# Two attention stages of a decoder step: the turns of the probabilities and the products with the values, spread over other slots of a round

## What is computed

```
# group B (MLA), sample: all 2048 cached latents (128 wide) and rotary keys (32 wide), and the 8 new ones
s = (einsum('bqhr,bkr->bhqk', ql, c_kv) + einsum('bqhd,bkd->bhqk', qp, k_pe)) * scale
p = softmax(where(key_pos <= q_pos, s, -inf));  o_lat = einsum('bhqk,bkr->bqhr', p, c_kv)
# group A (DSA), sample: an indexer scores the keys, each query keeps its best 256
score = einsum('bqh,bqhk->bqk', w_idx, relu(einsum('bqhd,bkd->bqhk', q_idx, k_idx)))
_, sel = top_k(score, 256)
p = softmax(einsum('bqhd,bqkd->bqhk', q, k[sel]) / 8);  o_a = einsum('bqhk,bqkd->bqhd', p, v[sel])
```

## Time and profile before

| what | us |
|---|---|
| median of three runs | 3161.12 |
| the profiled execution | 3156.46 |
| its span, first to last instruction | 3154.7 |
| PE busy | 2939.6 (93%) |
| DVE busy | 1413.7 (45%) |
| ACT busy | 998.4 (32%) |
| POOL busy | 643.3 (20%) |

### The profile page before, as it was taken

One profiled execution on the slowest core, in us unless ns is written; L12 is line 12 of the kernel. 1 busy time (PEld: TensorE's weight loads), 2 busy tenths in 40 slices (PEclk: granted clock), 3 DMA queues, 4 the chain that ended last, 5 costly groups with the idle time before them and its releaser, 6 DMA issues. The chain is left out here.

```text
span 3154.7 us, 45592 instructions
## 1 busy us (share of the span) xinstructions
PE 2939.6 (93%) x18282; PEld 2524.9 (80%) x18298; DVE 1413.7 (45%) x2118; ACT 998.4 (32%) x1620; POOL 643.3 (20%) x562
## 2 busy tenths in 40 slices
PE   7999999888898899999999999998888988999997
PEld 7999879755566689998799997795656666999975
DVE  2222255579764442223632223735887445222236
ACT  2222233454443332222422222334444333122223
POOL 1111021330113141110221110412302123211103
PEclk9999999999999999999999999999999999999998
DMA  4222452400123322224422224423002234222243
GB/s 118 80 80 80 134 158 79 144 1 1 68 86 131 107 87 80 80 80 135 160 87 80 80 86 141 144 62 134 1 18 80 74 113 147 73 80 79 88 147 124
DMA packets 241737, 293.79 MB, mean 93 GB/s; under 512 B 12624, under 2 KB 205488, under 8 KB 235456
## 3 DMA queue, kind: packets, MB, share of 16 engines
q1 hardware_dynamic: 234688, 229.00, 23.6%
q0 software_dynamic: 6912, 62.92, 5.4%
HBM read 287.72 MB, written 3.88 MB: 92 GB/s over the span
## 5 line engine op out<-in xcount | busy, mean ns | idle before, releaser
L159 DVE TENSOR_TENSOR wlo<-raw,whi 128x1024 fp32r<-128x1024 f32 (+2 forms) x398 | 515.0, 1295 | 1298.1 <-ACT whi L153 1296.9
L153 ACT ACTIVATE whi<-raw 128x1024 fp32r<-128x1024 f32 (+2 forms) x398 | 418.6, 1053 | 1438.7 <-PE ps L608 864.8
L608 PE MATMUL ps<-xth,whi 128*128 128x296 f32 x2624 | 752.2, 299 | 5.4 <-PEq L770 5.4
L608 PE MATMUL ps<-xtl,whi 128*128 128x296 f32 x2624 | 754.7, 300 | 0.0
L608 PE MATMUL ps<-xth,wlo 128*128 128x296 f32 x2624 | 571.7, 300 | 0.0
L608 PEld LDWEIGHTS ps<-xth,whi 128*128 128x128 f32 x2624 | 494.7, 189 | 5.5 <-issue 5.5
L608 PEld LDWEIGHTS ps<-xtl,whi 128*128 128x128 f32 x2624 | 493.5, 188 | 0.0
L608 PEld LDWEIGHTS ps<-xth,wlo 128*128 128x128 f32 x2624 | 427.5, 188 | 0.0
L166 PE MATMUL ps<-whi,hth 128*128 128x512 f32 (+1 forms) x880 | 350.6, 398 | 10.0 <-DVE wlo L159 8.4
L168 PE MATMUL ps<-whi,htl 128*128 128x512 f32 (+1 forms) x880 | 346.9, 394 | 0.0
L167 PE MATMUL ps<-wlo,hth 128*128 128x512 f32 (+1 forms) x880 | 346.7, 394 | 0.0
(11 more groups left out here) (407 smaller groups left out, 4348.0 us busy)
## 6 DMA issues: line engine op xcount, KB each, us to landing
raw<-in_ffn_w_in SPq DMA_DIRECT2D x176, 512.0 KB, 3.8
raw<-in_ffn_w_out SPq DMA_DIRECT2D x176, 512.0 KB, 3.5
raw<-in_w_o SPq DMA_DIRECT2D x32, 512.0 KB, 3.4
raw<-in_w_in SPq DMA_DIRECT2D x16, 507.0 KB, 3.9
gb<-in_ln_g SPq DMA_DIRECT2D x6, 512.0 KB, 5.6
gb<-in_ln_b SPq DMA_DIRECT2D x6, 512.0 KB, 6.4
raw<-in_w_in SPq DMA_DIRECT2D x8, 338.0 KB, 3.1
x<-in_x_prompt SPq DMA_DIRECT2D x1, 1536.0 KB, 10.7
```

The costliest lines, as they stand in the source:

```text
L153: e.activation(dst, T.raw[:, s, 0:width], ACT.Copy).then_inc(S.hi_done, 1)
L159: e.tensor_tensor(w_lo, T.raw[:, s, 0:width], w_hi.bitcast(F32), ALU.subtract).then_inc(S.split_done, 1)
L608: mm = e.matmul(bank(u, up)[:, h, :], part[:, s, w], xp[:, k, o], start=(k == 0 and part is T.whi and xp is T.xth), stop=(k == KD - 1 and ...
```

## The change

Two lists are replaced. One fifth is turned in each of slots 0 to 4 instead of five in slots 0 to 2, and the ten products stand in slots 1 to 7 instead of 1 to 6. Everything that goes by these lists moves with them: the list `order` of the two banks, the copies on ACT and DVE, and the moments at which `v_done` rises. Work and operands are the same.

```
--- before.py
+++ after.py
@@ -2218,8 +2218,8 @@
 
 
 
-    TURN = [(0, 1), (2,), (3, 4), (), (), (), (), ()]
-    VALUES = [(), ((0, 0), (0, 1)), ((0, 2), (0, 3), (0, 4)), ((1, 0),), ((1, 1),), ((1, 2),), ((1, 3), (1, 4)), ()]
+    TURN = [(0,), (1,), (2,), (3,), (4,), (), (), ()]
+    VALUES = [(), ((0, 0),), ((0, 1),), ((0, 2),), ((0, 3), (0, 4)), ((1, 0), (1, 1)), ((1, 2), (1, 3)), ((1, 4),)]
     O_SLOT = 3
 
     def turned_in(p, j):
```

## The result

| | before | after |
|---|---|---|
| median of 18 runs each, us | 3159.6 (3155.52 to 3165.68) | 3170.3 (3162.39 to 3174.72) |
| ratio, 95% interval | | 1.0031 (1.0024 to 1.0037): slower |
| span of the profiled execution, us | 3154.7 | 3170.7 |
| mean granted clock in it | 0.981 | 0.978 |

A forecast was written before the change was run, and what follows sets the result against it. TensorE, busy 93% of the span, was taken as the bound. Per layer D 2.4 + 0.4 and M 0.25 + 0.2 - 0.35 + 0.25 gave 3.15 us; two layers, 6.3, on 3161.12 gave 3167.4; 8-in-10 range 3159 to 3174.

The forecast's parts named there:

- The stall in D: D rounds 1 to 3: TensorE waits 1.55 us for a late low key part; each round 0.8 us longer.
- M rounds: M rounds 1, 2 and 3: three small terms, +0.25, +0.2 and -0.35 us.
- DVE's steps: M round 1: reordered selection steps leave VectorE no idle time before the maximum; some 0.2 us longer.
- the loads: M: page loads of sequences 4 and 6 start later; 0 to 0.35 us late in two rounds.
- The last rounds: Last round of each stage: copies behind other work, more changes between turns and products; +0.25 us in M, +0.4 in D.
- rival 1: Last rounds: shorter wait removes the half-speed stretch, about 1.6 us four times; time stays at 3161; chance 0.2.
- rival 2: D rounds: no stall at the second sequence's first turn, each round 0.74 us shorter; 3158.2 us; chance 0.1.
- 4: M: page loads take 9 to 10 us, making work 2.5 to 3.5 us late four times; 3178 to 3182; chance 0.07.
- 3: D rounds: the stall makes TensorE's clock fall, 1.6 us six times on top; 3177 us; chance 0.08.

The follow-up runs named there:

- experiment 1: Changed kernel, but in D rounds 1 to 3 ACT issues the high key part of the second sequence ahead of the copies: 3160.44 us, ratio 0.9993.
- experiment 4: Kernel before, with the high key part of the second sequence in D rounds 1 to 3 put into slot 2, behind the chunk's copy: 3170.28 us, ratio 1.0037.
- experiment 5: Kernel before, with only a pair's last product moved behind the last scores in D and M: one execution, 3171.11 us.
- experiments 6, 7 and 9: Transposes added ahead of the stages' last rounds: kernel before 3161.29 us; changed kernel 3160.52; new lists in D alone with high key part first 3154.03.
- D only: New lists in the D stage alone, the old ones in M, against the kernel before: 3166.95 us, ratio 1.0019.

## Why the prediction was right or wrong

Right on the side and by its main mechanism; the loss came out higher, +10.7 us in the first set (+8.6 by the table's means) where +6.3 was forecast. Some of the closeness in absolute time, 3170.3 for 3167.4, is luck: the sum was laid on 3161.12, the median of three runs of before, and eighteen gave 3159.6. The chances leaned slightly the other way (0.50 for no change, 0.45 for slower).

*The stall in D.* T1 starts 1.95 into the round (2.05 forecast), high at 3.14 (3.19 by the 1.05 later), k12 at 6.76 (6.83) after 1.45 us idle (1.55), the last scores at 17.10 (17.21). A round is 0.70 longer, for 0.8; without the stall 0.79 shorter, for 0.74 (experiment 1). Undoing the order on ACT takes the loss away, making it in the kernel before brings one (experiment 4): this step is shown. *M rounds.* +0.23, +0.18, -0.28 for +0.25, +0.2, -0.35. The load came at 18.81 us behind the round's exponential (forecast 877.4 - 858.6 = 18.8) and high waits for the DMA, as written. The round's end still hangs on DVE; experiment 5 gives V14 some 0.1 of the two gains in length, which the prediction gave to DVE's steps and the loads alone.

*The last rounds.* At the full level +0.54 in D and +0.13 in M, for +0.4 and +0.25; the wait of V04 behind the output's share is there with 0.51. With the rounds that makes 2.08 + 0.54 + 0.13 + 0.13 = 2.9 us a layer, 5.8 for both, against 6.3 in the sum. Each term of the sum was right to half a microsecond. The fit gives +4.4 for this part, 1.4 less.

*The step that failed* is that the sum had no term for the clock. "So a wait of 1.5 us was borne here at the full level, and I take the new stall of 1.55 as borne too" holds for the rounds themselves (1.00 from 989 to 1048). The Trainium skill (TensorE: Matmul & The Clock Gate, section A second HAM failure mode: psum-queue depth-cycling) tells of a kernel whose short idle times between groups of matmuls made the clock swing between its levels. The D rounds here do not show that swing: two waits a round after the change (1.13 and 1.45 us), four in experiment 4 (1.48, 0.35, 0.50 and 1.10), and 1.00 throughout in both.

But the last round was costed as if its half level stayed as it was in the earlier trace rows, and rival 1 let it only vanish. It grew: D's last rounds of the changed kernel had 6.8, 6.8, 6.8 and 0 us at half in two profiles, where before had 3.4 and 3.4 in one, and the time per run went up by 4.2 us with a mean clock of 0.9779 instead of 0.9795.

Rival 1 reckoned with a wait of 2.1 us in place of 2.5 in all four last rounds; it became 2.24 in D (from 2.50) and 1.96 in M (from 2.31), and the half level followed all ten M last rounds with 1.95 or 1.96 and eleven of the twelve D last rounds with 2.24 or 2.25. It followed none of the twelve with a fill and a wait of 0.06 to 0.51 (experiments 6, 7 and 9). After the change, layer 0 of M, PE and then a window:

```profile
955.26 1.06 PE L2400 MATMUL ps<-ident,MP 128*128 128x128 f32 x8 [1.96 <-ACT MP L2570]
956.67 1.97 PE L2417 MATMUL ps<-pg,MPT 128*64 128x128 f32 x8 [0.35 <-DVE MPT L2496]
...
956.60:959.80 3.20, 3.13 (x13) 2.47 (x14) 0.09 (x2) 0.36 (x1) 0.00 (x0) 0.50 0.74 309
```

With the fill the changed kernel's clock is 0.9807, and 8.1 of its 8.6 us are gone, 7.2 of them with the clock. By the mean clocks the changed kernel spends some 10 us more at half a run (0.0016 x 3165 / 0.5, an estimate); the last rounds of D can hold 6.8 of that if both have the longer kind. Where the rest falls is open: in the twelve profiles the part before the first M exponential holds from 34.1 to 47.8 us of half level and the part between the layers' sample stages from 37.5 to 51.2, though no kernel changes a line of either, so single profiles can't place it. Nor do the parts add up: 5.8 us by the rounds and 4.2 by the clock are more than the 8.6 measured. D only kept the clock of before (0.9795), which remains unexplained beside the changed kernel's 0.9779.

*The rivals.* 1 did not happen: in the two profiles of the changed kernel seven of the eight last rounds kept a half-level stretch. 2 (no stall) and 4 (slow loads, all 6.3 to 6.6) did not happen either; 4 comes to 3177.4 to 3181.4 by its own terms, for 3178 to 3182. 3 (the clock falls in D's rounds) did not: those rounds kept 1.00. The longer half level came in the round behind them. The rounds without the stall are worth what rival 2 said, once the order on ACT is changed.

## What to carry to other kernels

When a producer moves to a later slot, walk every in-order queue that its consumer stands in: what stands behind the consumer there is delayed too, though it shares no data with it, and the remedy is to issue that work ahead of the wait. Cost a stretch at the half clock as something that can come, go or double, and compare kernels at equal granted clock: here a fit on each run's mean clock brought the standard deviation from 3.3 us to 1.5, but left errors of up to 3 us between kernels. Before an idle time of TensorE is filled, look at the next one: the half level may turn up there, and then the fill pays only in part.

## What was not expected of the hardware

The same 2.25 us wait was followed by the half level in one layer and by the full one in the other of one execution (1.94 and 1.06 us for the same eight transposes). Behind that wait the half level lasted 6.8 us in four of six last rounds that follow the new stall, and 3.4 in all six that do not, though the stalled rounds themselves ran at 1.00. With such waits filled, 1.5 us were saved in each of four last rounds and 1.8 of each 3.0 lost again in D's first round, which then ran in part at 0.50. And 858 us of identical instructions took from 857.7 to 864.1 us in the profiles, with 34.1 to 47.8 us of them at half.
